# The last matrix of a feed-forward part as seven block products, gathered over three pieces of the inner dimension

## What is computed

```python
def conv_ffn(h, w_up, conv_w, conv_b, w_down):
    L = h.shape[1]
    z = h @ w_up                                       # 512 tokens x 1024 -> 5632
    ...                                                # width-3 convolution over the tokens
    gate, val = jnp.split(z, 2, axis=-1)
    return (jax.nn.gelu(gate) * val) @ w_down          # 512 x 2816 -> 512 x 1024
...
    f = conv_ffn(h, ffn_w_up[l], ffn_conv_w[l], ffn_conv_b[l], ffn_w_down[l])
    x = x + rms_norm(f, norm_ffn_post[l])
```

## Time and profile before

| | us |
|---|---|
| median of 3 runs | 3635.55 |
| lowest and highest | 3635.37, 3637.25 |
| the profiled execution, own time | 3641.15 |
| span of its trace | 3639.6 |
| TensorE busy (matmuls) | 3272.2, 90% of the span |
| VectorE, ScalarE, GpSimd busy | 1533.5, 794.7, 793.1 |
| mean granted TensorE clock | 0.937 |

### The profile page before, as it was taken

How to read it: one execution, slowest core, us unless ns; L and a number is a source line. 1 busy time by engine, 2 the same in 40 slices (tenths; PEclk the granted TensorE clock), 3 DMA queues, 4 the chain that set the end, 5 groups by cost and what they waited for, 6 DMA issues and landing times. The chain is left out here.

```text
span 3639.6 us, 36988 instructions
## 1 busy us (share of the span) xinstructions
PE 3272.2 (90%) x14152; PEld 2235.6 (61%) x14152; DVE 1533.5 (42%) x2641; ACT 794.7 (22%) x1756; POOL 793.1 (22%) x504
## 2 busy tenths in 40 slices
PE   6989999969998798999997899949799899699997
PEld 5858767734444585776665444428476666588843
DVE  4574712331111666476654011153676522555502
ACT  3362211021111245322322111111221111111100
POOL 3314122310000430401013000014344222253300
PEclk9989999979999898999999999969798789899999
DMA  3241222138887120132233788832101122112220
GB/s 144 72 194 70 93 77 85 64 134 319 323 324 275 63 93 24 47 116 104 93 122 122 267 324 323 316 141 76 49 24 48 48 93 93 47 70 93 105 80 23
DMA packets 50373, 471.13 MB, mean 129 GB/s; under 512 B 5713, under 2 KB 6097, under 8 KB 26513
## 3 DMA queue, kind: packets, MB, share of 16 engines
q1 hardware_dynamic: 26784, 378.70, 28.8%
q0 software_dynamic: 20816, 76.03, 5.3%
q10 hardware_dynamic: 2592, 13.93, 1.0%
HBM read 507.70 MB, written 63.70 MB: 157 GB/s over the span
## 5 line engine op out<-in xcount | busy, mean ns | idle before, releaser
L597 PE MATMUL bank<-B,ring 128*128 128x256 f32 x4336 | 957.8, 382 | 40.1 <-PEq L2084 10.0
L597 PEld LDWEIGHTS bank<-B,ring 128*128 128x128 f32 x4336 | 828.4, 191 | 166.1 <-issue 51.6
L1888 PE MATMUL bank<-ring,B 128*128 128x512 f32 x1024 | 452.2, 600 | 1.8 <-issue 1.6
L581 POOL TENSOR_TENSOR ring<-ring 128x1024 f32<-128x1024 f32 x52 | 132.8, 2553 | 1201.6 <-DMA ring<-in_w_static 319.7
L725 ACT ACTIVATE B<-bank 128x256 f32<-128x256 f32 x356 | 136.1, 384 | 1008.4 <-PE bank L597 982.4
L597 PE MATMUL bank<-XT,ring 128*128 128x256 f32 x1344 | 307.0, 383 | 43.7 <-PEq L813 28.9
L1888 PEld LDWEIGHTS bank<-ring,B 128*128 128x128 f32 x1024 | 193.9, 192 | 237.8 <-issue 235.6
L597 PEld LDWEIGHTS bank<-XT,ring 128*128 128x128 f32 x1344 | 257.5, 192 | 84.8 <-issue 49.9
L506 PE MATMUL bank<-B,ring 128*128 128x512 f32 x704 | 307.3, 596 | 2.0 <-issue 2.0
L1958 DVE TENSOR_TENSOR B<-B,bank 128x512 f32<-128x512 f32 x46 | 31.6, 687 | 492.3 <-PE bank L1888 480.2
L506 PEld LDWEIGHTS bank<-B,ring 128*128 128x128 f32 x704 | 134.5, 191 | 164.3 <-issue 163.4
(11 more groups left out here) (463 smaller groups left out, 4015.7 us busy)
## 6 DMA issues: line engine op xcount, KB each, us to landing
ring<-in_w_expert SPq DMA_DIRECT2D x96, 2048.0 KB, 9.2
ring<-in_w_static SPq DMA_DIRECT2D x79, 2048.0 KB, 8.0
B<-in_w_expert SPq DMA_DIRECT2D x42, 2048.0 KB
slots_y<-B POOLq DMA_DIRECT2D x53, 512.0 KB, 27.1
B<-slots_x POOLq DMA_DIRECT2D x46, 512.0 KB
slots_x<-B POOLq DMA_DIRECT2D x23, 512.0 KB, 16.1
ring<-s_tables SPq DMA_DIRECT2D x4, 2048.0 KB, 8.7
s_tables<-tmp POOLq DMA_DIRECT2D x8, 512.0 KB, 3.8
```

The lines of the kernel that those rows point to most:

```text
L581: pool.tensor_tensor(s(0), w(1, 0), w(1, 1), ALU.add).then_inc(made.up(), 1)
L597: ins = pe.matmul(out, left, right, start=start and k == 0, stop=k == 3, skip_group_check=not start)
L1888: ins = pe.matmul(bank[:, :], xbT[q % 2][:, k, :], slot[:, k, :], start=k == 0, stop=k == KT - 1)
```

## The change

`ffn_down` also goes by seven products. The list of names gets a `sums_ffn_down` behind each of the six `ffn_down` chunks, which are now cut as 1024 input by 512 output channels: three pieces of the inner dimension (8, 8 and 6 tiles) for each of the two halves of the output channels. Unlike `ffn_up`, each of the seven products has a bank of its own (both 128-channel parts side by side in it, 2 x 256 tokens), in which it gathers over the three pieces; ACT and DVE combine the banks only once for each output half. DVE makes four token sums for each piece, twelve in all.

```diff
 def is_split(name):
-    return name[0] in SPLIT or name[0] == "in2" and name[2] != 4
+    return name[0] in SPLIT or name[0] == "ffn_down" or name[0] == "in2" and name[2] != 4
...
+class DownProducts(SevenProducts):
+
+    PIECES = (4, 4, 3)
+    ORDER = ("first", "second", "fifth", "sixth", "seventh", "fourth", "third")
...
+            for at, kind in enumerate(self.ORDER):
+                self.bk.plan(("fd", o, kind), (7 * o + at) % 8)
...
+    def sum_hidden(self, dve, c):
+        made, x, T = self.m.tally("token_sums"), lambda k, h: self.hidden(c, k, h), lambda q: self.sums_of_tokens(c, q)
+        dve.tensor_tensor(T(0), x(0, 1), x(0, 0), ALU.subtract).then_inc(made.up(), 1)
+        dve.wait_ge(*made.at(4 * c + 1))
+        dve.tensor_tensor(T(1), x(1, 1), T(0), ALU.subtract).then_inc(made.up(), 1)
+        dve.tensor_tensor(T(2), x(1, 1), x(0, 1), ALU.subtract).then_inc(made.up(), 1)
+        dve.wait_ge(*made.at(4 * c + 2))
+        dve.tensor_tensor(T(3), x(1, 0), T(1), ALU.subtract).then_inc(made.up(), 1)
+
+    def accumulate(self, pe, o, c):
...
+        def product(kind, w, t):
+            key = ("fd", o, kind)
+            if c == 0:
+                pe.wait_ge(*bk.vacant(key))
+            bank, steps = bk.bank(key), self.PIECES[c]
+            for i in range(2):
+                out, part = bank[:, HALF * i:HALF * i + HALF], slice(i * P, (i + 1) * P)
+                for k in range(steps):
+                    ins = pe.matmul(out, w[:, k, part], t[:, k, :], start=c == 0 and i == 0 and k == 0, stop=c == 2 and i == 1 and k == steps - 1,
+                                    skip_group_check=True)
...
+        pe.wait_ge(*m.landed(self.names[n]))
+        product("first", self.w(n, 0, 0), x(0, 0))
+        product("second", self.w(n, 0, 1), x(1, 0))
+        pe.wait_ge(*weights.at(4 * n + 1))
+        pe.wait_ge(*tokens.at(4 * c + 1))
+        product("fifth", self.s(n, 0), T(0))
+        pe.wait_ge(*weights.at(4 * n + 2))
+        pe.wait_ge(*tokens.at(4 * c + 2))
+        product("sixth", self.s(n, 1), T(1))
+        pe.wait_ge(*weights.at(4 * n + 4))
+        pe.wait_ge(*tokens.at(4 * c + 3))
+        product("seventh", self.s(n, 2), T(2))
+        pe.wait_ge(*tokens.at(4 * c + 4))
+        raw = product("fourth", self.w(n, 1, 1), T(3))
...
+        summed = product("third", self.s(n, 3), x(1, 1))
...
+    def combine(self, dve, o):
...
+        add_bank("second", self.dest(o, 0, 0), upper_right)
+        add_bank("sixth", upper_right, upper_right)
...
+        add_bank("seventh", lower_right, upper_right)
...
+        dve.tensor_tensor(upper_right, upper_right, self.fifth_copy(o), ALU.add).then_inc(step.up(), 1)
+        added = step.last()
+        add_bank("fourth", self.dest(o, 1, 0), lower_right)
+        dve.wait_ge(*bk.read_done(("fd", o, "fourth")))
+        dve.tensor_tensor(lower_right, lower_right, self.fifth_copy(o), ALU.add).then_inc(step.up(), 1)
+        dve.wait_ge(*added)
+        add_bank("third", upper_right, upper_right)
...
 def ffn_down(m):
...
         @block.tensor
         def _(pe):
-            for k in range(FF_T):
-                name = ("ffn_down", 0, k // 4)
-                pe.wait_ge(*m.landed(name))
...
-                    ins = pe.matmul(bank[:, :], slot(k % 4, c), hidden_tile(m, k), start=k == 0, stop=k == FF_T - 1)
...
+            for o in range(2):
+                for c in range(3):
+                    seven.accumulate(pe, o, c)
+
+        @block.gpsimd
+        def _(pool):
+            for n in range(6):
+                seven.sum_weights(pool, n)
+
+        @block.scalar
+        def _(act):
+            for o in range(2):
+                seven.keep(act, o)
 
         @block.vector
         def _(dve):
-            for c in range(KT):
-                dve.wait_ge(*bk.made(("fd", c)))
-                bank = bk.bank(("fd", c))
-                dve.tensor_copy(m.B[1][:, c, :], bank[:, :]).then_inc(bk.free_sem(("fd", c)), 1)
+            for c in range(3):
+                seven.sum_hidden(dve, c)
+            for o in range(2):
+                seven.combine(dve, o)
```

More of the change, by code:

```diff
@@ L3080, in ffn_down @@
 def ffn_down(m):
-    bk = m.banks
     with m.stage() as block:
-        for c in range(KT):
-            bk.plan(("fd", c))
+        seven = DownProducts(m)
         @block.tensor
         def _(pe):
-            for k in range(FF_T):
-                name = ("ffn_down", 0, k // 4)
-                pe.wait_ge(*m.landed(name))
[L3092 to L3095, removed]
-                    bank = bk.bank(("fd", c))
-                    ins = pe.matmul(bank[:, :], slot(k % 4, c), hidden_tile(m, k), start=k == 0, stop=k == FF_T - 1)
[L3098 to L3103, removed]
+            for o in range(2):
+                for c in range(3):
+                    seven.accumulate(pe, o, c)
@@ L3253, in _static_chunks @@
         elif kind == "ffn_down":
-            w = i["ffn_w_down_2"][0][512 * j:512 * j + 512]
-            out.append(_tall(np.concatenate([w, np.zeros((512 - w.shape[0], D), np.float32)], 0)))
+            w = i["ffn_w_down_2"][0][1024 * (j % 3):1024 * (j % 3) + 1024, 512 * (j // 3):512 * (j // 3) + 512]
+            if j % 3 == 2:
+                gap = np.zeros((P, 512), np.float32)
+                w = np.concatenate([w[:3 * P], gap, w[3 * P:], gap], 0)
+            out.append(_wide(w))
     return np.stack(out)
```

47 lines of the change are left out of this document (added).

## The result

| | before | after |
|---|---|---|
| median of five runs, us | 3636.53 (3635.37 to 3642.76) | 3610.56 (3603.72 to 3621.9) |
| ratio to before, 95% interval | | 0.9934 (0.9916 to 0.9951) |
| profiled execution, its span | 3641.15, 3639.6 | 3610.05, 3608.5 |
| first matmul of `ffn_down` | 3460.46 | 3446.50 |
| from there to the start of the norm | 155.00 | 136.94 |

The change makes the kernel 0.66% faster, 26 us by the medians. I forecast 18.2 us. The range, 3613.5 to 3623, lies above the measured 3610.56.

A forecast was written before the change was run, and what follows sets the result against it. ffn_down was taken as bound by an unbroken row of TensorE matmuls: record count times pitch, plus slow-clock loss. Its part falls from 154.0 to 135.8 us, so 3635.55 − 18.2 = 3617.3 us, range 3613.5 to 3623.

The forecast's parts named there:

- Matmuls removed and added: In ffn_down, 352 records of 430 ns give way to 616 of 216 ns; TensorE's part falls 18.2 us.
- The pitch taken from `ffn_up`: Time per matmul record in ffn_down, claimed equal to that of ffn_up with the same shape: 216.0 ns.
- the 2.7 us for the clock: At ffn_down's start, work lost to the slow clock after the barrier's idle time: 2.7 us, unchanged, 0.5 to either side.
- Every cover: In ffn_down, weight sums, token sums and weight loads were each claimed hidden behind the matmuls, costing nothing.
- the ring: ffn_down's weight loads: hidden, narrowest case 8 us to spare; as rival, TensorE starves for loads, 3645.8 us, 2 in 100.
- Bank hand-over and end: Between ffn_down's output halves no wait; at its end one 0.69 us addition replaces a copy, change nothing, bounds −0.2 and +1.5.
- The late POOL: Rival at ffn_down's start: POOL's weight sums wait behind twelve token sums; gain 9.3 us, total 3626.3, 5 in 100.
- the time ahead of the stage: Stages before ffn_down: no reason seen for their time to move, so no change was counted.
- The uncertainty: For the whole kernel's runs, about 1.5 us from their spread of 1.9; with term bounds, 3614.5 to 3620.5 us.
- The clock held: Rival: the clock does not hold; with all of ffn_down at 1.2 GHz another 133 us, total 3750, 1 in 100.
- small waits: Rival: missed waits at product seams or in DVE's combination of the first half, 3 to 11 us, 5 in 100.

The follow-up runs named there:

- the halves: Kernel before, ffn_down matmuls of all 22 inner tiles, or of eleven, split into two of 256 tokens: medians 3629.78 and 3632.79 us; with eleven 3634.73 and 3630.29.
- doubled sums: Changed kernel, with four more POOL additions ahead of the four weight sums of ffn_down chunks 2 to 5: median 3606.11 us, ratio 0.9921.
- forced: Changed kernel, with POOL's first weight sum made to wait until all twelve token sums are made: median 3618.72 us, ratio 0.9954.
- padded: Kernel before, with 528 or 1056 one-column memsets of an unused buffer added on POOL: medians 3634.07 us (ratio 1.0004) and 3640.28 us (1.0012).
- wider input: Kernel before, with one small input made twice as wide by 32 KB of zeros never read: median 3633.95 us, ratio 0.9998.
- variants: Changed kernel with POOL waiting for all token sums, with extra POOL additions, or with ffn_down drawn into ffn_up's stage: medians 3618.72, 3606.11, 3598.92 us.

## Why the prediction was right, and where it was wrong

**Matmuls removed and added: right.** 154.0 us of TensorE were forecast to become 135.8; 135.84 were measured. The pitch taken from `ffn_up` and the 2.7 us for the clock both hold, and the halves show the shape to cost 0.6 us, 0.7 in their repeat.

**Every cover held.** TensorE's only wait in the stage is the barrier. POOL's first eight sums took 3.2 to 3.4 us, the later sixteen 2.35, and doubled sums changed nothing. The token sums ended near 30 us into the stage instead of 35, since DVE's last three ran alone at 0.95. The static loads of this time landed after 7.5 to 8.8 us, so the ring was even easier than I had it.

**Bank hand-over and end: right.** The last addition is 0.69 us and the norm starts 1.1 us behind the last matmul.

**The late POOL** was put at 9.3 us of gain left, that is 8.9 lost; forced, it lost 7.4, the wait 5.76 where I had 6.2 and the clock 1.6 where I had 2.7. I had weighed there the rule of the Trainium skill, page "SBUF — State Buffer", section "Who interferes with whom", that the engine which issues second is blocked for a whole instruction of the other. The trace bears the exclusion out nearly: alone a token sum takes 1.22 us and a weight sum 2.35, together 3.57, and side by side one pair of them takes about 3.3. But the block ends with the instruction, and the engines take turns, so POOL was never held behind all twelve.

**What failed is a term put at nothing: the time ahead of the stage.** The forecast moved the total by the stage's 18.2 us alone, and the prediction says of the time before the stage that it saw no reason for it to move. It did move. Against the mean of the kernel before, the changed kernel gains 3635.0 − 3609.3 = 25.7 us, standard error 1.4, where the stage has 18.1. With the clock taken out it gains 23, so about 5 us are gained ahead of the stage, in code that did not change. The other 2.7 us go with a somewhat higher clock in these 17 executions, 0.9394 against 0.9385 on average, and may be chance. Of the 5 us about 3 are shared with the halves, whose TensorE program is also longer and whose weights also land 0.3 us sooner, and about 2, with a standard error of 0.7, are the changed kernel's own.

**The uncertainty was too small as well**, "about 1.5 us, by their spread of 1.9". Three runs that lie within 1.9 us were no measure of the spread: 109 executions of that kernel reach from 3622.7 to 3646.2. Attention and mixer run between both levels of the clock, 1.2 and 2.4 GHz, and the share of each differs from execution to execution. I read the clock only at the two places where it bore on my sum. In the first trace the two attentions and the mixer, at 0.80, 0.79 and 0.85, hold about half of the time that the kernel spends at the lower level (0.937 over the span). A median of five, with a standard deviation of some 5 to 6 us, is uncertain by about 3 us, so a range of 9.5 us that also held the bounds of all terms was too narrow. But the spread does not account for the miss by itself: the mean of 17 executions, 3609.3 with a standard error of 1.4, is outside the range of 3613.5 to 3623 too, and so is that of the 11 among them without the doubled sums, 3610.8. Of the 13.96 us by which the first two traces differ ahead of the stage, the larger part can be chance, for the kernel before differed from itself by 9.3.

**The other rivals.** The clock held at 1.00 and the ring never starved, so the side on which it would have been slower had nothing to it. No small waits were missed.

**Open.** Why a longer TensorE program lets the static weights land 0.3 us sooner, whether that is what makes the earlier stages shorter, and why the changed kernel gains more there than the halves. The two projections of qkv show where about half of it lies. In these stages the only waits of TensorE that the profile names are for additions on DVE (L696), and POOL, which works beside DVE, waits for the loads. Both projections together, in us, over all traces:

```
kernels                                   both projections   of it waits for DVE
before, padded, wider input (5 traces)    303.6 to 305.1     4.5 to 6.8
halves (4)                                302.6 to 306.0     4.1 to 5.8
changed kernel and its variants (5)       300.8 to 302.7     2.4 to 4.2
```

The changed kernel and its variants are 2.5 us shorter here than the first group in the mean. The halves are no shorter in the mean (304.3 in both), though their weights land as early. So an early landing alone does not shorten the projections, and what the changed program has beyond that is not known. Where in memory the weights lie was only tried with one input.

## What to carry to other kernels

A gapless stage on TensorE is priced by the number of records, the pitch of a twin stage with the same shape, and the work of each other engine against the time in which it is wanted; done so, it came out to 0.2 us. The total is another matter. Before a range is given for it, look at the granted clock of every stage in which TensorE stops and starts, for most of the scatter between executions goes with it, and three runs that agree do not measure it. When two kernels are compared, compare them at an equal mean clock too: here that took half of the scatter away. And leave room for code that did not change: it gave about 5 us here. And a barrier ahead of a full stage costs twice, once as idle time and once in the clock behind it; drawing the two stages together gave another 10 us here.

## What the runs showed of the hardware that I had not expected

- The same loads of 2 MB land after 8.0 to 8.1 us (median of 79) in five traces of one group of programs and after 7.7 to 7.8 in nine traces of another, without overlap. The groups differ in the length of TensorE's program; 528 or 1056 instructions more on POOL did not have that effect.
- One kernel's executions differ by 23 us, 0.6%, with nothing changed, and its attention stage by 6 us of 96, with the clock at 0.80 or 0.89. Over 104 executions the mean granted clock and the time have a correlation of −0.85.
- After 5.76 us of waiting in mid-stage TensorE lost 1.6 us to the 1.2 GHz level; after the barrier's 7.33 us, 2.7.
